# Sum of squares over channels in two fp32r parts, placed behind the first added products; one output product of the last head placed behind that head's own sum

## The chip, the cores and the metric

The kernel is one program on one core of a Trainium2 chip. The metric is the device time of that program in microseconds (us): the median of several runs. Engines are named as in the profile: PE (TensorE, matmuls), PEld (its weight loads, which run beside the matmuls), DVE (VectorE), ACT (ScalarE), POOL (GpSimd), SP (the queue that issues loads).

## The reference, cut to what matters

Two transformer-like blocks in fp32 over x with 1024 tokens and 1024 channels.

```
x = x + concat(pool_mixer, hgrn2_mixer) @ w_out            # first block
h = rms_norm(x, g);  x = x + square(relu(h @ w_up)) @ w_down
x = x + merged @ w_out                                     # second block
h = rms_norm(x, g);  up = dwconv3(h @ w_up);  x = x + (gelu(gate) * val) @ w_down
rms_norm(x, g) = x * rsqrt(mean(x*x over channels) + eps) * g
```

The mean is over channels. Channels lie on the 128 partitions (8 tiles of them), so the squares are first added over the 8 tiles and then over the partitions, by a product with a matrix of ones.

## The kernel before

Each fp32 product is made of three fp32r products: with w = w_hi + w_lo and a = a_hi + a_lo (the high part is a copy into fp32r, the low part the rest of it), PE adds w_hi*a_hi, w_hi*a_lo and w_lo*a_hi in PSUM. ACT makes the high parts of activations, DVE the low parts; for the weights ACT makes high parts and POOL the low ones. Each engine works through an order written out by hand and waits on counting semaphores.

Both up-projections (called stages `mlp` and `ffn`, each one a call of `up_stage` on PE and of `enter` on ACT and DVE) use a Strassen-like scheme: for each pair of output tiles, seven products (`b11, t2, t3, t1, b21, t4, b22`) of 4 row pairs kk, that is 12 matmuls of 128x512 each, so 84 matmuls for a pair. The row pairs are taken in PAIR_ORDER = (0, 1, 3, 2). The factors of h are in part direct (DIRECT: b11, t1, b21, b22) and in part sums (MIXED: t2, t3, t4); each has a sum by DVE, a high part by ACT (`h_combo_hi`, L2402) and a low part by DVE (`h_lows`, L3326 and L3328). The high part of "y" (`..._t_scaled`) is the scaled term from which DVE's three mixed sums (L3310, L3313, L3315) start.

The scale 1/rms is not in h: it is multiplied in when results are read. DVE's first reads of the results (`first_pieces`, L3451; `first_ffn_pieces`, L3809) need it as `rinv`.

The entry of a stage, that is its first pair (`first_pair` on PE), is made of plain products, since the sums are not there yet:
- PE: `begin`/`end` of b11 in banks 6 and 7, `begin` of t1 in banks 0 and 1, then **`sum_features`** (L1482: ones times `sq_sum`, plain fp32, two halves, into banks 4 and 5), then two `add_product`s of 12 matmuls each, then `end`, `add_product`, `end`, `add_product` (30 matmuls), and then pair 2 (`up_pair`), whose b11 waits for `piece_read` (both first pieces read out of banks 6 and 7) and for the low part of its a11.
- ACT (`enter`): last square, `first_sum`, `second_sum`, the high parts of row pair 3 MIXED (y, t2, t3, t4), y of row pair 2, then `inverse` (waits for `norm_summed`; Ln at L2205 out of banks 4 and 5, Exp at L2207, each with a table load ahead of it), then the high parts t2, t3, t4 of row pair 2, then the high parts of pair 2's weights (L2420).
- DVE (`enter`): last addition of squares (L3340), then sums and low parts MIXED of row pair 3, then of row pair 2, then the first pieces.
- POOL (`split_pair`): sums of pair 2's weights (L1294 to L1304), then their low parts (L1318), each behind its high part.

In stage `ffn` DVE also handles the width-3 convolution of the pair before (`tap`, L3839 and L3843), the gelu product (`gated`, L3849) and reads the t1 piece at L3897; PE's last product of a pair, b22, goes into the same bank as t1 and so waits for that read.

The last head (`head(HEADS - 1, ...)`) runs steps of the recurrence, with products of the output projection between them (`begin_out(t, [k])`: output tile t, channel tile k, 6 matmuls of 128x512). Its mean of squares is already made in two fp32r parts: sq_hi by ACT (L2366), sq_lo by DVE (L3270), four matmuls (L1649) behind a wait for `sq_lo_ready`; ACT takes Ln of it (L2368, `o_log`), and the third output tile (`begin_third`) waits for that, as its banks are those of the mean.

`sq_hi_ready` and `sq_lo_ready` are one counter each for the whole program: 6 heads, then two more in the layer norm of the second block.

## Time and profile before

| | us |
|---|---|
| median of 3 runs | 2427.71 (2427.33 to 2430.54) |
| the profiled execution | 2425.44 |
| its span | 2423.6 |

In the page of the profile:

| engine | busy us | share |
|---|---|---|
| PE | 2399.5 | 99% |
| PEld | 1978.9 | 82% |
| DVE | 1890.3 | 78% |
| POOL | 1361.3 | 56% |
| ACT | 959.4 | 40% |

A matmul of 128x512 in fp32r is listed with 389 ns, but consecutive ones start closer together than that, since they are pipelined. In a timeline a row gives the start, the length, the engine, the line, what it writes and reads, and in brackets how long the engine was idle before it and what ended that. In the chain of waits a row gives the start and length of a stretch and what it was spent on.

### The profile page before, as it was taken

The numbers are of one execution on the slowest core, as the hardware profiler recorded it, in microseconds if no ns is written. First come the engines' busy times: TensorE is split into PE (matmuls) and PEld (weight loads), VectorE is DVE, ScalarE is ACT, GpSimd is POOL, SyncE is SP. The second block draws the span as 40 slices with busy tenths as digits, with TensorE's granted clock in tenths as the row PEclk, the third lists the DMA queues.
The fourth block names the chain that finished last, engine by engine and source line by source line (L and its number), as shares of the span: only waits on it lengthen the run. The fifth ranks groups of instructions, "written<-read, shape, count | busy, mean of one in ns | idle before, by whom it ended". The sixth has DMA issues, their size and how long they took to land.

```text
span 2423.6 us, 37422 instructions
## 1 busy us (share of the span) xinstructions
PE 2399.5 (99%) x13845; PEld 1978.9 (82%) x13845; DVE 1890.3 (78%) x1915; ACT 959.4 (40%) x1318; POOL 1361.3 (56%) x792
## 2 busy tenths in 40 slices
PE   8999999999999999999999999999999999999998
PEld 8788887888888788887777788888888888888887
DVE  6766666776667788888877889354799999999998
ACT  5344445353333533324333331310355455443434
POOL 3222222369887767772322223333379999978786
PEclk9999999999999999999999999999999999999999
DMA  6111112234444755431311111113222222235332
GB/s 227 37 35 43 35 35 97 105 122 160 148 155 171 258 172 155 151 126 37 130 42 35 39 35 52 44 52 123 95 87 78 87 86 87 78 129 184 105 118 88
DMA packets 243637, 244.79 MB, mean 101 GB/s; under 512 B 16944, under 2 KB 212187, under 8 KB 238811
## 3 DMA queue, kind: packets, MB, share of 16 engines
q1 hardware_dynamic: 214916, 166.70, 22.1%
q10 hardware_dynamic: 28630, 76.86, 8.3%
q8 instruction: 59, 0.97, 0.2%
q14 instruction: 32, 0.25, 0.0%
HBM read 181.13 MB, written 64.17 MB: 101 GB/s over the span
## 4 chain that ended last, share of the span: by engine, by line
PE 86%; DVE 7%; POOL 2%; ACT 2%; issue 2%; DMA 1%; SPq 0%; DVEq 0%; POOLq 0%; ACTq 0%
PE psum L1455 30%; PE psum L1744 26%; PE psum L1864 11%; PE psum L2112 7%; PE psum L2014 3%; PE psum L1493 2%; PE psum L1580 1%; PE psum L1518 1%; PE psum L1926 1%; PE psum L1945 1%; DVE sq_sum_gain L3583 0%; POOL ffn_s_lo L1318 0%; PE psum L1640 0%; DVE sq_sum L3340 0%; DVE sq_sum L3574 0%
## 5 line engine op out<-in xcount | busy, mean ns | idle before, releaser
L1261 POOL CAST w_hi<-w_raw 128x1024 fp32r<-128x1024 f32 x85 | 98.2, 1156 | 770.3 <-issue 386.4
L1455 PE MATMUL psum<-h_hi,w_hi 128*128 128x512 f32 x1040 | 329.7, 398 | 0.6 <-DVE zg L3074 0.3
L1455 PE MATMUL psum<-h_lo,w_hi 128*128 128x512 f32 x1040 | 321.4, 390 | 0.0
L1455 PE MATMUL psum<-h_hi,w_lo 128*128 128x512 f32 x1040 | 320.7, 390 | 0.0
L1455 PEld LDWEIGHTS psum<-h_hi,w_lo 128*128 128x128 f32 x1040 | 195.2, 188 | 41.9
L1455 PEld LDWEIGHTS psum<-h_lo,w_hi 128*128 128x128 f32 x1040 | 195.2, 188 | 41.6
L1269 POOL TENSOR_TENSOR w_lo<-w_raw,w_hi 128x1024 fp32r<-128x1024 f32 x85 | 221.0, 2601 | 9.6 <-DVE h_lo L3043 2.8
L1455 PEld LDWEIGHTS psum<-h_hi,w_hi 128*128 128x128 f32 x1040 | 189.2, 188 | 38.9 <-issue 2.1
L3637 DVE SCALAR_TENSOR_TENSOR conv_t<-u_t,cols,conv_t 128x1024 f32<-128x1024 f32 x120 | 175.2, 1460 | 2.6
L1318 POOL TENSOR_TENSOR ffn_s_lo<-ffn_s_sum,ffn_s_hi 128x512 fp32r<-128x512 f32 x84 | 159.8, 1931 | 7.0 <-POOL ffn_s_sum L1304 3.5
L1744 PE MATMUL psum<-ffn_t_hi,ffn_s_hi 128*128 128x512 f32 x252 | 98.0, 389 | 0.0
L1744 PE MATMUL psum<-ffn_t_lo,ffn_s_hi 128*128 128x512 f32 x252 | 98.0, 389 | 0.0
L1744 PE MATMUL psum<-ffn_t_hi,ffn_s_lo 128*128 128x512 f32 x252 | 98.0, 389 | 0.0
L1318 POOL TENSOR_TENSOR mlp_s_lo<-mlp_s_sum,mlp_s_hi 128x512 fp32r<-128x512 f32 x60 | 94.9, 1611 | 2.7 <-ACT mlp_s_hi L2420 2.7
L1864 PE MATMUL psum<-down_part_hi,down_hi_odd 128*128 128x512 f32 x228 | 88.8, 390 | 0.3 <-DVE down_x L3501 0.3
L1864 PE MATMUL psum<-down_part_lo,down_hi_odd 128*128 128x512 f32 x228 | 88.7, 389 | 0.0
L1864 PE MATMUL psum<-down_part_hi,down_lo_odd 128*128 128x512 f32 x228 | 88.7, 389 | 0.0
L3493 DVE TENSOR_TENSOR down_part_lo<-down_part_raw,down_part_hi 128x1536 fp32r<-128x1536 f32 (+2 forms) x31 | 71.0, 2291 | 8.5 <-ACT down_part_hi L2556 8.5
L1864 PE MATMUL psum<-down_part_hi,down_hi_even 128*128 128x512 f32 x196 | 76.2, 389 | 0.0
L1864 PE MATMUL psum<-down_part_lo,down_hi_even 128*128 128x512 f32 x196 | 76.2, 389 | 0.0
L1864 PE MATMUL psum<-down_part_hi,down_lo_even 128*128 128x512 f32 x196 | 76.2, 389 | 0.0
L2420 ACT ACTIVATE ffn_s_hi<-ffn_s_sum 128x512 fp32r<-128x512 f32 x84 | 48.4, 624 | 63.8 <-POOL ffn_s_sum L1296 55.7
(626 smaller groups left out, 6857.3 us busy)
## 6 DMA issues: line engine op xcount, KB each, us to landing
w_raw<-in_w_in SPq DMA_DIRECT2D x120, 256.0 KB, 3.0
w_raw<-in_w_up SPq DMA_DIRECT2D x76, 256.0 KB, 3.4
act_parts<-act_mixed ACTq DMA_DIRECT2D x15, 1024.0 KB, 3.8
down_part_raw<-act_parts SPq DMA_DIRECT2D x14, 1024.0 KB, 5.6
down_part_raw<-act_parts SPq DMA_DIRECT2D x15, 768.0 KB, 6.4
ffn_raw<-in_w_up SPq DMA_DIRECT2D x44, 256.0 KB, 3.5
ffn_rows<-ffn_gate ACTq DMA_DIRECT2D x22, 512.0 KB, 2.6
ffn_part_raw<-ffn_rows SPq DMA_DIRECT2D x18, 512.0 KB, 4.5
```

Of the source, the lines that this page charges most:

```text
L1261: pool.tensor_copy(hi, raw).then_inc(weight_hi, 1)
L1269: pool.tensor_tensor(lo, raw, hi.bitcast(F32), ALU.subtract).then_inc(weight_split, 1)
L1318: done = pool.tensor_tensor(lo[:, :], full[c], hi[:, :].bitcast(F32), ALU.subtract)
L1455: last = pe.matmul(psum[:, first_bank + t, :], w, a[:, k, t * HALF:(t + 1) * HALF], start=(k == order[0] and j == 0), stop=(k == order[-1] ...
L1493: last = pe.transpose(psum[:, dst_bank + c // 4, (c % 4) * P:(c % 4 + 1) * P], block_in, ident[:, :])
L1744: last = pe.matmul(psum[:, bank, :], w, a[:, :], start=start and kk == part[0] and j == 0, stop=stop and kk == part[-1] and j == 2, skip_g ...
L1864: done = pe.matmul(psum[:, bank, :], w, b, start=first and i == 0 and k == 0, stop=last and i == len(window) - 1 and k == 2)
L2014: last = pe.matmul(psum[:, bank + t, :], w, a[:, t * HALF:(t + 1) * HALF], start=(k == 0 and j == 0), stop=(k == 3 and j == 2))
L2112: done = pe.matmul(psum[:, bank, 0:tokens.stop - tokens.start], w, b, start=first and i == 0 and k == 0, stop=last and i == len(window) - ...
L2420: act.activation(stage.weights[s][c][0][:, :], src, ACT.Copy).then_inc(weight_combo_hi, 1)
L3493: dve.tensor_tensor(part_lo[f % 3][:, here, :], part_raw[f % 3][:, here, :], part_hi[f % 3][:, here, :].bitcast(F32), ALU.subtract).then_i ...
L3637: dve.scalar_tensor_tensor(acc, u_t[:, c % 2, tap:tap + SEQ], w, acc, ALU.mult, ALU.add)\
```

## The change

- `first_pair` (both stages): `sum_features` is taken out. Behind the two `add_product`s, PE waits for `sq_lo_ready` and makes four fp32r matmuls of `norm_ones` with `norm_hi` and `norm_lo` (two halves each) into the same banks 4 and 5.
- ACT, in `enter`: behind the MIXED high parts of row pair 3 it copies ones into `norm_ones` (128x128) and `sq_sum` into `norm_hi` (128x1024, fp32r); then y of row pair 2 and `inverse` as before.
- DVE, in `enter`: behind the MIXED sums and low parts of row pair 3 it waits for `sq_hi_ready` and makes `norm_lo` = `sq_sum` - `norm_hi` (128x1024), then the MIXED part of row pair 2 as before. `norm_hi` lies where `rinv` lies, `norm_lo` where `sq_sum` lies, `norm_ones` in the free bytes at the end.
- Last head: the product of output tile 1, channel tile 6, is made at the start of `begin_third`, behind the four matmuls of the head's own mean, and not ahead of them.
- Later waits on the two shared counters are raised by the numbers added (`sum_channels`, `out_scaled`, the layer norm).

```diff
@@ buffers
+        norm_ones = at("norm_ones", [P, P], A_END, F32R)
+        norm_hi, norm_lo = (at(f"norm_{n}", [P, SEQ], a, F32R) for n, a in (("hi", A_CONST + 4 * KB), ("lo", A_NORM + 24 * KB)))
@@ PE, last head
             def begin_third():
+                begin_out(1, [6])
                 begin_out(2, range(7))
...
-                             lambda: begin_both((1, 5), (0, 6), (1, 6)), begin_third, lambda: begin_both((1, 0), (0, 1))])
+                             lambda: begin_both((1, 5), (0, 6)), begin_third, lambda: begin_both((1, 0), (0, 1))])
@@ PE, first_pair
                 begin(stage, "a21", "t1", 0)
                 begin(stage, "a11", "t1", 1)
-                sum_features(sq_sum, stage.sums + KT - 1, 4)
                 pe.wait_ge(weight_combo, q * 7 + 7)
                 pe.wait_ge(first_taken, q + 1)
                 add_product(stage, "a12", "b21", 6).then_inc(seventh_done, 1)
                 pe.wait_ge(sum_taken, q * 2 + 2)
                 add_product(stage, "a22", "b21", 7).then_inc(seventh_done, 1)
+                pe.wait_ge(sq_lo_ready, HEADS + (1 if stage is mlp else 4))
+                for j, part in enumerate((norm_hi, norm_lo)):
+                    for t in range(2):
+                        last = pe.matmul(psum[:, 4 + t, :], norm_ones[:, :], part[:, t * HALF:(t + 1) * HALF],
+                                         start=j == 0, stop=j == 1)
+                last.then_inc(norm_summed, 1)
                 end(stage, "a21", "t1", 0)
@@ ACT, enter
                 h_combos_hi(stage, PAIR_ORDER[2], MIXED)
+                act.activation(norm_ones[:, :], ones[:, :], ACT.Copy)
+                act.activation(norm_hi[:, :], sq_sum[:, :], ACT.Copy).then_inc(sq_hi_ready, 1)
                 h_combo_hi(stage, PAIR_ORDER[3], "y")
                 inverse(m, norm, eps)
@@ DVE, enter
-                for kk in PAIR_ORDER[2:]:
-                    h_combos(stage, kk, MIXED)
+                h_combos(stage, PAIR_ORDER[2], MIXED)
+                dve.wait_ge(sq_hi_ready, HEADS + (1 if stage is mlp else 4))
+                dve.tensor_tensor(norm_lo[:, :], sq_sum[:, :], norm_hi[:, :].bitcast(F32), ALU.subtract).then_inc(sq_lo_ready, 1)
+                h_combos(stage, PAIR_ORDER[3], MIXED)
```

## Rows read from the trace of the kernel before

**Rows 1.** The page: granted clock of PE in 40 slices of the span.
```profile
PEclk9999999999999999999999999999999999999999
```
**Rows 2.** Chain of waits, whole span: start us, us, what.
```profile
420.29 68.34 PE psum L1455 x300
488.63 9.52 PE psum L1744 x42
498.15 1.72 PE psum L1482 x4
499.87 284.30 PE psum L1744 x1254
...
1838.81 345.75 PE psum L1744 x1524
```
**Rows 3.** Timeline, end of the last head: ACT, DVE and PE.
```profile
416.25 1.28 ACT L2368 ACT_TABLE_LOAD   x1
416.26 1.23 DVE L3270 TENSOR_TENSOR sq_lo<-e_t,sq_hi 128x1024 fp32r<-128x1024 f32 x1 [5.86 <-ACT sq_hi L2366]
418.02 0.62 PE L1649 MATMUL psum<-sq_hi,ones_r 128*128 128x512 f32 x2
418.47 0.61 PE L1649 MATMUL psum<-sq_lo,ones_r 128*128 128x512 f32 x2
419.13 1.11 ACT L2368 ACTIVATE e_t<-psum,eps 128x1024 f32<-128x1024 f32 x1 [1.60 <-PE psum L1649]
420.29 0.74 PE L1455 MATMUL psum<-h_hi,w_out_hi 128*128 128x512 f32 x2 [1.21 <-ACT e_t L2368]
```
**Rows 4.** Timeline, entry of stage mlp, ACT.
```profile
501.29 0.63 ACT L2402 ACTIVATE mlp_t_hi<-mlp_t_sum 128x512 fp32r<-128x512 f32 x1 [0.55 <-DVE mlp_t_sum L3315]
501.82 0.71 ACT L2402 ACTIVATE mlp_t_scaled<-x_t,cols 128x512 f32<-128x512 f32 x1
...
503.85 1.12 ACT L2205 ACTIVATE rinv<-psum,eps 128x1024 f32<-128x1024 f32 x1
```
**Rows 5.** Timeline, entry of stage mlp, DVE.
```profile
501.23 2.88 DVE L3326 TENSOR_TENSOR mlp_t_lo<-mlp_t_sum,mlp_t_hi 128x512 fp32r<-128x512 f32 x3
504.03 0.74 DVE L3310 SCALAR_TENSOR_TENSOR mlp_t_sum<-x_t,cols,mlp_t_scaled 128x512 f32<-128x512 f32 x1
...
507.96 1.90 DVE L3326 TENSOR_TENSOR mlp_t_lo<-mlp_t_sum,mlp_t_hi 128x512 fp32r<-128x512 f32 x3 [1.62 <-ACT mlp_t_hi L2402]
509.77 1.28 DVE L3451 SCALAR_TENSOR_TENSOR mlp_a<-psum,rinv 128x512 f32<-128x512 f32 x2
```
**Rows 6.** Timeline, entry of stage mlp: POOL, and PE's first matmul of pair 2.
```profile
500.59 1.76 POOL L1304 TENSOR_TENSOR mlp_s_sum<-mlp_raw,mlp_s_sum 128x512 f32<-128x512 f32 x1
509.57 1.44 POOL L1318 TENSOR_TENSOR mlp_a_lo<-mlp_raw,mlp_a_hi 128x512 fp32r<-128x512 f32 x1 [7.22 <-ACT mlp_a_hi L2420]
...
511.99 0.39 PE L1744 MATMUL psum<-mlp_b_hi,mlp_a_hi 128*128 128x512 f32 x1
```
**Rows 7.** Groups by line and shape, ACT: the copy of ones elsewhere.
```profile
L2743 ACT ACTIVATE ln_ones<-ones 128x128 fp32r<-128x128 f32 x1 | 0.3, 290 | 0.0
```
**Rows 8.** Timeline, entry of stage ffn: DVE and ACT.
```profile
1774.92 0.74 DVE L3310 SCALAR_TENSOR_TENSOR ffn_t_sum<-x_t,cols,ffn_t_scaled 128x512 f32<-128x512 f32 x1
...
1774.74 1.12 ACT L2205 ACTIVATE rinv<-psum,eps 128x1024 f32<-128x1024 f32 x1
```
**Rows 9.** Timeline, stage ffn, DVE's t1 reads of pairs 3 to 5, and PE.
```profile
1816.73 0.67 DVE L3897 TENSOR_TENSOR ffn_z_val<-third_sum,psum 128x512 f32<-128x512 f32 x1
...
1838.08 0.68 DVE L3897 TENSOR_TENSOR ffn_z_val<-third_sum,psum 128x512 f32<-128x512 f32 x1
...
1856.79 0.67 DVE L3897 TENSOR_TENSOR ffn_z_val<-third_sum,psum 128x512 f32<-128x512 f32 x1
...
1838.81 0.50 PE L1744 MATMUL psum<-ffn_b_hi,ffn_s_hi 128*128 128x512 f32 x1 [1.44 <-DVE ffn_z_val L3897]
```
**Rows 10.** Timeline, stage ffn: DVE's gelu product of the pair before.
```profile
1819.62 2.26 DVE L3849 TENSOR_TENSOR ffn_gate<-ffn_gate,ffn_val 128x1024 f32<-128x1024 f32 x1 [1.61 <-ACT ffn_gate L2802]
```

More of the change, by code:

```diff
@@ L570, in out_scaled @@
             done = {"act": tile_scaled, "dve": out_ready, "pool": pool_scaled}[by]
-            eng.wait_ge(done, (KT if by == "pool" else HEADS + 2) + OUT_BY[:t + 1].count(by))
+            eng.wait_ge(done, (KT if by == "pool" else HEADS + 4) + OUT_BY[:t + 1].count(by))
         psum = ctx.enter_context(nc.psum_tensor("psum", [P, BANKS, HALF], F32))
@@ L2032, in sum_channels @@
             def sum_channels(hi, lo, nth, first_bank, done):
-                pe.wait_ge(sq_lo_ready, HEADS + nth)
+                pe.wait_ge(sq_lo_ready, HEADS + 1 + nth)
                 for j, part in enumerate((hi, lo)):
@@ L3736, in _ @@
                                   ALU.add).then_inc(ln_added, 1)
-            dve.wait_ge(sq_hi_ready, HEADS + 1)
+            dve.wait_ge(sq_hi_ready, HEADS + 2)
             dve.tensor_tensor(ln_sum_lo[:, :], ln_inv[:, :], ln_sum_hi[:, :].bitcast(F32), ALU.subtract).then_inc(sq_lo_ready, 1)
@@ L3748, in _ @@
                 dve.tensor_tensor(ln_sq[0], ln_sq[0], ln_sq[c], ALU.add).then_inc(ln_added, 1)
-            dve.wait_ge(sq_hi_ready, HEADS + 2)
+            dve.wait_ge(sq_hi_ready, HEADS + 3)
             dve.tensor_tensor(ln_sq_lo[:, :], ln_sq[0], ln_sq_hi[:, :].bitcast(F32), ALU.subtract).then_inc(sq_lo_ready, 1)
```

## The prediction

> **What bounds the kernel now.** I read four views in this order. The chain of waits over the span shows where one engine sets the end: from the end of the last head to deep in stage mlp it is PE alone, product after product, with the fp32 sum as a link of its own [rows 2], and from 1838.81 on the same in stage ffn. In such a stretch a microsecond taken from PE is a microsecond gained, and one of idle PE is lost. 42 products take 9.52 us, so one takes 0.227; 1254 in 284.30 give the same [rows 2]. The timeline around the last head shows a PE that waits 1.21 us for ACT's Ln [rows 3]. The timelines of the two entries show what ACT, DVE and POOL have ready, and when [rows 4 to 8]. The last is stage ffn's pairs 3 to 5: before 1838.81 PE does not set the end there; it waits 1.44 us for DVE's t1 read [rows 9].
>
> **Last head.** Nothing is removed: six matmuls, 6 x 0.227 = 1.36 us, go behind the mean's four. The mean now starts at 418.02, when PE gets to it, though sq_lo is ready at 416.26 + 1.23 = 417.49 [rows 3]. Without the six ahead of it PE would be there at 416.66, so it waits for sq_lo instead and starts near 417.54. Starting again after a wait costs PE about 0.1 us: the two matmuls at 420.29, behind one, are listed with 0.74, those at 418.02, without one, with 0.62 [rows 3]. So Ln starts at 419.13 - 0.48 + 0.1 = 418.75 and ends at 419.87. PE fills that time with the moved product, until about 419.9. The third tile starts at 419.9, not 420.29: **-0.4 us**. Its bounds are 0 (the product's data is late and nothing moves) and -0.5 (no restart cost). The table load ahead of Ln stands at 416.25, right behind sq_hi, and Ln then waits 1.60 for PE: a load is done ahead of the wait [rows 3]. I need that below.
>
> **Entry of stage mlp.** *Removed:* the fp32 sum, 1.72 us of PE [rows 2]. *Added on PE:* four fp32r matmuls, 4 x 0.227 = 0.91. By itself that is -0.81.
> *The new wait.* PE now goes on to the two added products, 24 x 0.227 = 5.44 us, and is through at 498.15 + 5.44 = 503.6 (0.2 earlier for the start of the next, as a listed end lies behind the next start). Is norm_lo there? ACT's last high part of row pair 3 starts at 501.29, the next operation at 501.82 [rows 4]. There norm_ones begins (0.29, [rows 7]), then norm_hi, for which I take the 1.11 of an ACTIVATE of that width [rows 3]; norm_hi is done at about 503.2. DVE's low parts of row pair 3 run from 501.23 to 504.03 [rows 5], so norm_hi is in time and DVE sets it: norm_lo from 504.03 to 505.26, with sq_lo's 1.23 for the same shape [rows 3]. PE waits from 503.4 to 505.3, **1.9 us idle**. All of PE's later work of this entry stands behind that wait. The four matmuls end at 505.3 + 0.1 + 3 x 0.227 + 0.39 = 506.5; PE is free for the 30 remaining ones at 506.3 and would begin pair 2 at 506.3 + 30 x 0.227 = 513.1, where it was 511.99 [rows 6]: +1.1 already.
> *Who waits for the sum.* ACT's Ln starts at 503.85 now [rows 4], behind its table load, long after the sum. It will start at 506.5: its table load is done while it waits, as in the last head. That is 2.65 to 2.7 later. Behind Ln stand, in ACT's order, Exp, the high parts of row pair 2 and the high parts of pair 2's weights; so DVE's low parts at 507.96 [rows 5] and POOL's a11 low part at 509.57 [rows 6] come 2.7 later too. DVE's own new 1.23 is covered: its sums of row pair 2 move from 504.03 to 505.26, end by 507.6, and before they were followed by 1.62 us of waiting for ACT [rows 5]. If that cover were gone, 1.23 would be added once.
> *What PE meets at pair 2.* b11 needs both first pieces read: now at 509.77 + 1.28 = 511.05, then at 513.75 [rows 5]. It needs a11's low part: 509.57 + 1.44 = 511.01, then 513.7 [rows 6]. PE, there at 513.1, waits to 513.8 and restarts at about 0.1: 513.85 against 511.99, **+1.85 us**. After that PE is alone on the chain to 784 [rows 2], so nothing gives it back. Bounds: +1.0 (PE's own time, if the pieces came early enough) and +2.7 (all of ACT's delay).
>
> **Entry of stage ffn.** The same code, with the same distances: DVE is free for norm_lo at 1774.92, so it ends at 1776.15, the four matmuls near 1777.4, and Ln starts there, against 1774.74 [rows 8]: +2.7 for ACT, and +1.85 for PE at pair 2. But here PE is not what sets the end later. Pair 4's b22 waits until 1838.81 for a DVE that runs behind [rows 9], and that DVE is chained to ACT (1.61 us idle for the gelu [rows 10]), ACT to POOL's sums, and POOL to the high parts that stand behind Exp; through this run the 2.7 go on unreduced. PE alone would be at b22 at 1838.81 - 1.44 + 1.85 = 1839.2, the read is done at 1838.76 + 2.7 = 1841.5: the stage moves by **+2.7 us**, and PE's wait grows from 1.44 to 2.3. Bounds: +0.4 (DVE catches up all of it, 1.85 - 1.44) and +2.7 plus one more slow pair, which is a rival below.
>
> **Moved DMAs:** none; the change issues no transfer, and no queue is passed. The raised counts of later waits cost nothing: the same events release them. Banks 4 and 5 are first reused by the next stage's products.
>
> **The skill's price of a table load.** The rows show a load of 1.28 us and the next ACTIVATE at once behind it: Ln ends at 419.13 + 1.11 = 420.24, and such loads sit between Ln and Exp. The Trainium skill, ScalarE: Activation LUTs, "What ACT_TABLE_LOAD costs", puts about 1283 ns on the load and a further 1380 on a drain, 2.66 in all. By it a load hidden in the wait would hide twice as much and Ln's delay would be some 1.4 less in each stage. The load's 1283 ns agrees with this trace, the drain is not in it, and the sum goes by the trace.
>
> **Sum.** -0.4 + 1.85 + 2.7 = +4.15, call it +4.2 us. Against the profiled execution's own 2425.44 that is 2429.6. That execution was 2.3 under the median of the three runs; I carry the difference over to the median: 2427.71 + 4.2 = **2431.9 us**, +0.17%. A difference under 0.2% (4.9 us) can't be told from none here.
>
> **The rivals.**
> - *The sum is covered, and the gain is what PE saves.* Then PE gains 0.81 twice and 0.4 in the head: -2.0, 2425.7. It needs norm_lo at 503.4 instead of 505.26. For it: the last square sum is ready long before. Against it: DVE's own order, full from 501.23 to 504.03 [rows 5]. Chance 0.05.
> - *Stage ffn takes only what PE loses.* DVE catches up before pair 4; its pairs can take 18.7 us (1838.08 to 1856.79 [rows 9]) where PE's take 84 x 0.227 = 19.05, and with PE later DVE waits less for it. Then the stage costs +0.4 to +1.1 and the total is about +2.1, 2429.8. Against it: that idle time of 1.61 waits for ACT, not PE. Chance 0.17.
> - *Slower: the slow pair repeats.* Pair 3 to 4 took DVE 1838.08 - 1816.73 = 21.35 us, the next 18.7 [rows 9]; the difference, 2.6, is what DVE's two-input operations lose when they meet POOL's, together with the wait for the gelu [rows 10]. With ACT, DVE and POOL 2.7 later against PE, DVE's reads can fall behind a POOL operation for one pair more. It decides when the t1 read of pair 5 ends more than 19.05 us behind that of pair 4. Price +2.6: total +6.8, 2434.5. For it: DVE is busy throughout there, and the first low part of row pair 3 in [rows 5], three of which take 2.88 where three later ones take 1.90, loses 1.0 while POOL is in its 1.76 us operation at 500.59 [rows 6]. Against it: everything on these three engines shifts together, and POOL is idle from 502.35 to 509.57, around norm_lo. Chance 0.18. The Trainium skill, SBUF — State Buffer, "SBUF: two separate sides", says that a DVE operation with two SBUF inputs and a GpSimd one take a common port in turn, each for its whole length; the lost 1.0 agrees, and norm_lo is such an operation, so by that rule too it is the meeting that counts and not the work.
> - *The idle 1.9 us lowers PE's clock.* The granted clock is full in all 40 slices, the one with the 1.21 us wait among them [rows 1]. I give it less than 0.02 and put it into the slower side.
>
> **How the numbers follow.** Forecast 0.6, rivals 0.05, 0.17, 0.18. The forecast's own range is +3.2 to +5.4 (the two restarts, 0.2 on norm_lo's start, and a median of a few runs that itself moved by up to 3 us): 2430.5 to 2433.5. Its upper part passes 4.9, some 0.2 of the 0.6. So slower is 0.2 + 0.18 = 0.38, faster 0.03, same 0.59. For 8 in 10 the range goes down to the weaker stage ffn and up to the repeated slow pair: 2427.8 to 2434.8.
>
> **What would show it.** In the changed profile: four matmuls with norm_hi and norm_lo of 0.39 us each; PE idle some 1.9 us ahead of them in both stages, released by DVE norm_lo; norm_lo of 1.23 right behind the third low part; ACT's table load ahead of a wait of 1.4 us or so and Ln 2.7 later against the entry's start; a PE wait of about 0.7 at the first matmul of pair 2; in stage ffn a wait of 2 to 2.5 at pair 4's b22; in the last head the third tile 0.4 earlier. The forecast is wrong if PE finds norm_lo ready, if the wait at b22 of ffn's pair 4 has shrunk, or if a wait at L3897 shows up in pair 5.

## The result, and the profile after

The changed kernel took 2432.49 us (median of 10 runs, 2431.03 to 2435.53) against 2427.27 us of the kernel before in the same session (10 runs, 2425.13 to 2433.01): ratio 1.0023, 95% interval [1.0015, 1.0031], +5.2 us. The forecast was 2431.9 with a range of 2427.8 to 2434.8 and a difference of +4.2. The changed kernel, run a second time in a later session, gave 2432.15 against 2426.89 (1.0019 [1.0010, 1.0028]). So it is slower by about 5 us. The prediction drew the bound between "same" and "slower" at 0.2% (4.9 us), and both intervals contain it; the point of the ten runs is just beyond, on the side to which the prediction gave 0.38 and not 0.59.

In the one profiled execution of each, the span went from 2423.6 to 2430.5 us, +6.9. By marks that exist in both traces it comes about so:

| from the mark | to the mark | before | after | difference |
|---|---|---|---|---|
| start of the span | sq_lo of the last head | 416.26 | 417.30 | +1.04 |
| sq_lo | third output tile's first product | 4.03 | 3.71 | -0.32 |
| there | last addition of squares, stage mlp | 73.41 | 73.34 | -0.07 |
| there | PE's first product of pair 2, mlp | 18.29 | 20.63 | +2.34 |
| there | last addition of squares, stage ffn | 1252.59 | 1253.39 | +0.80 |
| there | b22 of pair 4, ffn | 74.23 | 77.31 | +3.08 |
| there | end | 584.79 | 584.82 | +0.03 |

The first row lies ahead of everything that was changed, and the fifth between the two entries, where the chain of waits after shows a transfer of activations for the down-projection (`down_part_raw<-act_parts`, 7.79 us at 789.99) that it does not show before. Neither came back in the experiments below in a fixed size (between the entries it is 1252.3 to 1254.9 us over all traces, 1252.6 before), so I don't count them to the change. The change's own three rows give -0.32 + 2.34 + 3.08 = **+5.1 us**, which agrees with the timed runs.

**The last head.** The timeline of the changed kernel (start us, us, engine, line, operation, and in brackets the idle time before it with what ended it), DVE, ACT and PE in turn:

```profile
417.30 1.22 DVE L3280 TENSOR_TENSOR sq_lo<-e_t,sq_hi 128x1024 fp32r<-128x1024 f32 x1 [5.86 <-ACT sq_hi L2374]
...
417.28 1.28 ACT L2376 ACT_TABLE_LOAD   x1
419.83 1.12 ACT L2376 ACTIVATE e_t<-psum,eps 128x1024 f32<-128x1024 f32 x1 [1.26 <-PE psum L1651]
...
418.58 0.74 PE L1651 MATMUL psum<-sq_hi,ones_r 128*128 128x512 f32 x2 [0.70 <-DVE sq_lo L3280]
...
421.01 0.71 PE L1457 MATMUL psum<-h_hi,w_out_hi 128*128 128x512 f32 x2
```

As in [rows 3], with everything 1.04 us later. PE now reaches the mean before sq_lo is there and waits 0.70 us; in return the moved product stands behind the mean and fills the time of Ln, and the 1.21 us wait ahead of the third tile is gone. The third tile comes 3.71 us behind sq_lo's start, where it was 4.03.

**Entry of stage mlp.** First the chain of waits of the changed kernel, from the third low part to pair 2 (start us, us, what):

```profile
501.28 0.64 ACT mlp_t_hi L2410
...
502.81 2.38 DVE mlp_t_lo L3336 x2
505.19 1.15 DVE norm_lo L3372
...
506.38 1.21 PE psum L1798 x4
...
507.62 1.12 ACT rinv L2213
...
513.63 1.21 DVE mlp_a L3463 x2
...
514.98 5.05 PE psum L1747 x21
```

In [rows 2] this stretch was PE alone. Now the chain leaves PE, runs over DVE's low parts to norm_lo, the four matmuls, ACT's Ln, back to DVE and only at 514.98 to PE again. The timeline of the same stretch, ACT:

```profile
501.28 0.63 ACT L2410 ACTIVATE mlp_t_hi<-mlp_t_sum 128x512 fp32r<-128x512 f32 x1 [0.55 <-DVE mlp_t_sum L3325]
501.82 0.29 ACT L2473 ACTIVATE norm_ones<-ones 128x128 fp32r<-128x128 f32 x1
502.02 1.04 ACT L2474 ACTIVATE norm_hi<-sq_sum 128x1024 fp32r<-128x1024 f32 x1
502.97 0.71 ACT L2410 ACTIVATE mlp_t_scaled<-x_t,cols 128x512 f32<-128x512 f32 x1
503.69 1.28 ACT L2213 ACT_TABLE_LOAD   x1
507.62 1.12 ACT L2213 ACTIVATE rinv<-psum,eps 128x1024 f32<-128x1024 f32 x1 [2.64 <-PE psum L1798]
```

DVE and POOL:

```profile
501.22 3.97 DVE L3336 TENSOR_TENSOR mlp_t_lo<-mlp_t_sum,mlp_t_hi 128x512 fp32r<-128x512 f32 x3
505.12 1.21 DVE L3372 TENSOR_TENSOR norm_lo<-sq_sum,norm_hi 128x1024 fp32r<-128x1024 f32 x1
...
511.73 1.90 DVE L3336 TENSOR_TENSOR mlp_t_lo<-mlp_t_sum,mlp_t_hi 128x512 fp32r<-128x512 f32 x3 [3.17 <-ACT mlp_t_hi L2410]
513.55 1.28 DVE L3463 SCALAR_TENSOR_TENSOR mlp_a<-psum,rinv 128x512 f32<-128x512 f32 x2
...
502.30 1.74 POOL L1306 TENSOR_TENSOR mlp_s_sum<-mlp_raw,mlp_s_sum 128x512 f32<-128x512 f32 x1
513.34 1.44 POOL L1320 TENSOR_TENSOR mlp_a_lo<-mlp_raw,mlp_a_hi 128x512 fp32r<-128x512 f32 x1 [9.30 <-ACT mlp_a_hi L2428]
```

and PE:

```profile
506.38 0.73 PE L1798 MATMUL psum<-norm_hi,norm_ones 128*128 128x512 f32 x2 [2.15 <-DVE norm_lo L3372]
506.95 0.63 PE L1798 MATMUL psum<-norm_lo,norm_ones 128*128 128x512 f32 x2
...
514.98 0.47 PE L1747 MATMUL psum<-mlp_b_hi,mlp_a_hi 128*128 128x512 f32 x1 [0.59 <-DVE mlp_a L3463]
```

Against [rows 4 to 6] three things are to be seen. The third group of low parts takes 3.97 us, not 2.88, since it meets one more of POOL's weight sums: POOL's last one stands at 502.30 where it was at 500.59, 1.71 later, of which the stage's own shift is 0.65. (norm_lo is late by less than the 1.1 us that the group is longer: counted from the last addition of squares, the group starts 0.66 earlier than before, since the first of DVE's three sums, 1.43 us before, now takes 0.75 and misses POOL.) norm_lo follows it, and PE, done with the added products, is idle 2.15 us for it. ACT has its table loaded by 504.97 and then waits 2.64 us: Ln, Exp, the high parts, POOL's and DVE's parts behind them all come 3.1 us later, and PE waits once more, 0.59, at pair 2.

**Stage ffn.** The same entry, and pair 4's b22, on PE:

```profile
1780.40 0.73 PE L1798 MATMUL psum<-norm_hi,norm_ones 128*128 128x512 f32 x2 [2.19 <-DVE norm_lo L3372]
...
1788.99 0.47 PE L1747 MATMUL psum<-ffn_b_hi,ffn_a_hi 128*128 128x512 f32 x1 [0.59 <-DVE ffn_z_val L3821]
...
1845.68 0.50 PE L1747 MATMUL psum<-ffn_b_hi,ffn_s_hi 128*128 128x512 f32 x1 [1.98 <-DVE ffn_z_val L3909]
```

and ACT's Ln and DVE's t1 reads of pairs 4 and 5:

```profile
1781.63 1.12 ACT L2213 ACTIVATE rinv<-psum,eps 128x1024 f32<-128x1024 f32 x1 [2.64 <-PE psum L1798]
...
1844.95 0.68 DVE L3909 TENSOR_TENSOR ffn_z_val<-third_sum,psum 128x512 f32<-128x512 f32 x1
...
1863.68 0.68 DVE L3909 TENSOR_TENSOR ffn_z_val<-third_sum,psum 128x512 f32<-128x512 f32 x1
```

The prediction's path to b22 can be read from the chain of waits of the kernel before, stage ffn (pieces of it; start us, us, what), with POOL's row of the changed kernel's timeline last:

```profile
1778.14 1.66 ACT ffn_t_hi L2402 x3
...
1780.47 1.45 POOL ffn_a_lo L1318
...
1818.54 1.05 ACT ffn_gate L2802
...
1787.36 1.43 POOL L1320 TENSOR_TENSOR ffn_a_lo<-ffn_raw,ffn_a_hi 128x512 fp32r<-128x512 f32 x1 [9.30 <-ACT ffn_a_hi L2428]
```

The chain goes from Ln over ACT's high parts to POOL, which from then on has hardly a gap, to ACT's gelu and DVE. From POOL's first low part to b22 it is 58.34 us before (1838.81 - 1780.47) and 58.32 after (1845.68 - 1787.36). Compared with [rows 9], b22's wait grew from 1.44 to 1.98, and the restart is 64.05 us behind Ln (1845.68 - 1781.63), as it was before (1838.81 - 1774.74 = 64.07): the delay of Ln arrives there unreduced. Pair 4 to pair 5 takes 18.73 us: there is no second slow pair.

### The profile page after: what moved, and what is told of

It reads as the page before. It is cut to its first block, busy times and chain, and to the rows that moved or that the text cites. A ratio compares the mean times of both kernels' runs of the same rounds, so it can differ in the third digit from the quotient of the medians.

```text
span 2430.5 us, 37428 instructions
## 1 busy us (share of the span) xinstructions
PE 2401.2 (99%) x13845; PEld 1980.5 (81%) x13845; DVE 1890.3 (78%) x1917; ACT 961.1 (40%) x1322; POOL 1362.1 (56%) x792
## 4 chain that ended last, share of the span: by engine, by line
PE 85%; DVE 9%; ACT 3%; issue 2%; DMA 1%; POOL 1%; SPq 0%; DVEq 0%; ACTq 0%; POOLq 0%
PE psum L1457 28%; PE psum L1747 27%; PE psum L1872 11%; PE psum L2120 7%; PE psum L2022 3%; PE psum L1495 2%; PE psum L1582 1%; PE psum L1520 1%; PE psum L1953 1%; PE psum L1934 1%; DVE sq_sum L3350 1%; DVE sq_sum_gain L3595 0%; PE psum L1642 0%; DVE x_t L3358 0%; DVE ffn_t_lo L3336 0%
```

## The experiments

"Marks" are distances in us from the start of the last addition of squares of a stage, so that the start of the run doesn't enter them. Each comes from one profiled execution. Of the kernels themselves:

| kernel | Ln mlp / ffn | pair 2 mlp / ffn | b22 (its wait) | difference of medians, ratio |
|---|---|---|---|---|
| before | 10.15 / 10.16 | 18.29 / 18.24 | 74.23 (1.44) | |
| changed | 13.27 / 13.26 | 20.63 / 20.62 | 77.31 (1.98) | +5.2, 1.0023 [1.0015, 1.0031] |

**The three parts of the change, each alone.** The first has the head's move only:

```diff
             def begin_third():
+                begin_out(1, [6])
                 begin_out(2, range(7))
...
-                             lambda: begin_both((1, 5), (0, 6), (1, 6)), begin_third, lambda: begin_both((1, 0), (0, 1))])
+                             lambda: begin_both((1, 5), (0, 6)), begin_third, lambda: begin_both((1, 0), (0, 1))])
```

> The kernel before with the last head's product moved, and nothing else. My theory: the head's mean starts when sq_lo is ready and not when PE gets to it, so ACT's Ln comes some 0.4 us earlier against the head's earlier steps and the third output tile starts 0.35 to 0.45 us earlier against sq_hi; PE waits about 0.7 us for sq_lo and no longer for Ln. Time: -0.4 us (2427.3 becomes 2426.9), ratio 0.9998. Rival (the restart and the later product take it all back): 0.0 us and the third tile no nearer to sq_hi.

The second and third have the sum in parts in one stage only (`if stage is mlp` or `if stage is ffn` around the copies, norm_lo and the four matmuls, the other stage keeping its fp32 sum), and no move in the head.

> The kernel before with the two-part sum in stage mlp alone; stage ffn and the head as before. My theory: PE idle about 2 us for norm_lo and 0.6 us at the first product of pair 2; that product starts 1.9 to 2.3 us later against the last addition of squares than before (18.3 us behind its start before), and stage ffn as before (1.4 us wait at pair 4's b22). Time: +1.9 to +2.3 us, ratio 1.0008 to 1.0010. Rival (stage mlp has slack behind the entry that takes it back): pair 2 starts 2 us later, the down-projection does not, 0 us.

> The kernel before with the two-part sum in stage ffn alone. My theory: the whole delay of ACT's Ln reaches the end, through POOL, ACT's gelu and DVE's t1 read: PE's restart at pair 4's b22 comes 2.7 to 3.1 us later against the last addition of squares (74.2 us behind its start before). Time: +2.7 to +3.1 us, ratio 1.0011 to 1.0013. Rival (only what PE loses counts): +1.0 us or less, the wait at b22 gone or shorter.

| kernel | Ln mlp / ffn | pair 2 mlp / ffn | b22 (its wait) | difference of medians, ratio |
|---|---|---|---|---|
| e1_head_only | 9.48 / 10.58 | 18.29 / 18.24 | 74.66 (1.86) | -0.5, 0.9998 [0.9989, 1.0007] |
| e2_mlp_only | 12.94 / 10.27 | 20.30 / 18.23 | 74.35 (1.55) | +2.2, 1.0007 [0.9998, 1.0016] |
| e3_ffn_only | 10.30 / 13.45 | 18.29 / 21.23 | 77.49 (1.70) | +3.1, 1.0013 [1.0004, 1.0022] |

The three add up to -0.5 + 2.2 + 3.1 = +4.8 of the +5.2. Each of these differences is known to some 2 us only, and those of e1 and e2 can't be told from no change; only e3's can. What speaks for the three terms is the marks: the third tile 3.68 us behind sq_lo instead of 4.03, pair 2 of stage mlp later by 2.0, b22 later by 3.3. That stage ffn costs more than stage mlp shows in the marks; the timed intervals of e2 and e3 overlap and don't show it.

The unedited entries in this table say how far one mark can be trusted. With the fp32 sum in its old place Ln stands anywhere from 9.48 to 10.58 and b22 from 74.23 to 74.66, so a mark of one trace is good to about half a us. And e3's pair 2 in stage ffn, 21.23 and without a wait, is not comparable with the changed kernel's 20.62: 0.6 us behind the restart at its four matmuls this execution has a stretch of half clock (last section), and from norm_lo to Ln it is 2.94 us where the changed kernel has 2.50.

**What is it in the entry: the place, the low parts, or the split?** This kernel is the one before with nothing split and no move in the head; only the fp32 sum is moved to where the change has it:

```diff
-                sum_features(sq_sum, stage.sums + KT - 1, 4)
                 pe.wait_ge(weight_combo, q * 7 + 7)
...
                 add_product(stage, "a22", "b21", 7).then_inc(seventh_done, 1)
+                sum_features(sq_sum, stage.sums + KT - 1, 4)
```

> The kernel before with the plain fp32 sum moved behind the two added products in both stages: no new wait, PE's work unchanged. My theory (the late Ln costs, not only PE's idle time): PE is not idle in the entry; the sum ends near 505.4 and Ln starts 1.6 us later than before; pair 2 of stage mlp starts 0.8 us later, stage ffn's b22 of pair 4 1.6 us later. Time: +2.4 us, ratio 1.0010. Rival (what costs is PE idle ahead of the new wait and nothing else): 0.0 us.

Measured: 2430.8 against 2427.43, +3.4, 1.0009 [1.0000, 1.0018]; Ln at 11.63 / 11.60, pair 2 at 18.98 / 18.95, b22 at 75.66 with a wait of 2.01. So moving the sum behind the added products alone delays Ln by 1.5 us, and by the marks it costs 0.69 at pair 2 of stage mlp and 1.43 at b22, +2.1, with no idle PE at the sum. That is less than half of the +5.4 (2.34 + 3.08) that the change costs in the two entries; the splitting, which was to make PE's part shorter, adds the rest. (The timed +3.4 is more than the marks give, as with e5 below; the last section comes back to it.)

The next keeps the changed kernel but takes norm_lo out of the way; PE waits for norm_hi and adds it twice:

```diff
-                pe.wait_ge(sq_lo_ready, HEADS + (1 if stage is mlp else 4))
-                for j, part in enumerate((norm_hi, norm_lo)):
+                pe.wait_ge(sq_hi_ready, HEADS + (1 if stage is mlp else 4))
+                for j, part in enumerate((norm_hi, norm_hi)):
...
-                dve.wait_ge(sq_hi_ready, HEADS + (1 if stage is mlp else 4))
-                dve.tensor_tensor(norm_lo[:, :], sq_sum[:, :], norm_hi[:, :].bitcast(F32), ALU.subtract).then_inc(sq_lo_ready, 1)
+                dve.sem_inc(sq_lo_ready, 1)
```

> The changed kernel without norm_lo: DVE does not make it, PE waits for norm_hi alone and adds it twice, so the mean that scales both stages' results is twice the sum of the high parts and not the sum. PE's four matmuls, ACT's two copies and the place of the sum are as in the changed kernel. My theory (the wait for norm_lo is most of the loss): norm_hi is ready 8.7 us behind the start of the last addition of squares, PE gets to the sum at 9.7, so it doesn't wait; Ln at 10.8 (13.3 in the changed kernel, 10.15 before), pair 2 of stage mlp at 18.05 (before 18.29), pair 4's b22 of stage ffn 0.65 later than before. Time: 0.0 us against before, ratio 1.0000. Rival (the added copies and the late place of the sum cost by themselves): +2 us or more.

Measured: 2428.96 against 2426.61, +2.35, 1.0008 [1.0000, 1.0017]. The interval just reaches no change, but the marks speak against the expected 0: Ln is at 11.31 / 11.46, pair 2 of stage mlp at 18.66 behind a wait of 1.09 (expected: 18.05), b22 at 75.52 (2.00). ACT's timeline of e5_no_low, stage mlp:

```profile
502.40 0.29 ACT L2473 ACTIVATE norm_ones<-ones 128x128 fp32r<-128x128 f32 x1
502.60 1.04 ACT L2474 ACTIVATE norm_hi<-sq_sum 128x1024 fp32r<-128x1024 f32 x1
503.55 0.71 ACT L2410 ACTIVATE mlp_t_scaled<-x_t,cols 128x512 f32<-128x512 f32 x1
504.27 1.28 ACT L2213 ACT_TABLE_LOAD   x1
505.57 1.12 ACT L2213 ACTIVATE rinv<-psum,eps 128x1024 f32<-128x1024 f32 x1
```

Nothing waits here. Ln is late by 1.2 us because the two new copies, from 502.40 to 503.55, stand ahead of it in ACT's own queue. Not all of the 1.2 is theirs, though: in e6 below ACT waits for PE and not for the copies, and Ln is at 10.82, 0.67 late by the place of the sum alone. The copies add some 0.5 to that. Where PE's wait goes, ACT's copies are next, and the stages are still slower than before. The prediction placed the copies in time, to see whether norm_hi is there for norm_lo, and put no price on these 1.15 us of ACT, on which everything behind Ln hangs; in the changed kernel the wait for norm_lo covers them.

**Is norm_lo late for its work or for meeting POOL?** The changed kernel, with POOL's weight sums of pair 2 held back until norm_lo is done:

```diff
+                    pool.wait_ge(sq_lo_ready, HEADS + (1 if stage is mlp else 4))
```

> The changed kernel, with POOL's weight sums of pair 2 held back until norm_lo is done. Theory (DVE is late with norm_lo because its mixed sums and low parts meet POOL's operations): DVE's sums take 0.75 each and not 1.67, its three low parts 1.9 and not 3.97, norm_lo starts 7.0 us behind the start of the last addition (10.8 in the changed kernel), PE doesn't wait, Ln at 10.8; POOL's sums end at about 15.1 and are in time for the high parts. Time: 0.0 us against before, ratio 1.0000. Rival (DVE's and ACT's own order sets norm_lo): norm_lo at 10 or later, +4 us or more.

Measured: 2427.51 against 2426.61, +0.9, 1.0001 [0.9993, 1.0010]: no slowdown can be told from none. DVE's timeline of e6_pool_held, stage mlp, and POOL's first sum:

```profile
498.13 0.75 DVE L3326 SCALAR_TENSOR_TENSOR mlp_t_sum<-x_t,cols,mlp_t_sum 128x512 f32<-128x512 f32 x1
498.96 1.90 DVE L3337 TENSOR_TENSOR mlp_t_lo<-mlp_t_sum,mlp_t_hi 128x512 fp32r<-128x512 f32 x3
501.06 1.23 DVE L3373 TENSOR_TENSOR norm_lo<-sq_sum,norm_hi 128x1024 fp32r<-128x1024 f32 x1 [0.20 <-ACT norm_hi L2475]
...
502.58 1.51 POOL L1297 TENSOR_TENSOR mlp_s_sum<-mlp_raw 128x512 f32<-128x512 f32 x1 [15.89 <-DVE norm_lo L3373]
```

DVE's sum at 498.13 takes 0.75 us where the changed kernel's same sum at 499.52 took 1.67, the three low parts 1.90 instead of 3.97, and norm_lo starts at 7.19 instead of 10.77. PE does not wait at the four matmuls; ACT waits 1.76 us for them ahead of Ln. Ln stands at 10.82 / 10.77, pair 2 at 18.18 / 18.13, b22 at 74.83 with a wait of 1.98. So PE gets back 0.1 us at pair 2, where it waits 0.59, and b22 is still 0.6 late. The rival that norm_lo is simply one operation too many on DVE falls.

**Versions that might beat both.** The first is the kernel before with the head's move and the fp32 sum one place *earlier*, between the two begun products, Ln and Exp ahead of row pair 3's mixed high parts (PAIR_ORDER[2] is row pair 3, where the expectation of e11_early_again says row pair 2). The head's part of the edit is e1's; the rest:

```diff
                 begin(stage, "a21", "t1", 0)
-                begin(stage, "a11", "t1", 1)
                 sum_features(sq_sum, stage.sums + KT - 1, 4)
+                begin(stage, "a11", "t1", 1)
...
-                h_combos_hi(stage, PAIR_ORDER[2], MIXED)
-                h_combo_hi(stage, PAIR_ORDER[3], "y")
+                h_combo_hi(stage, PAIR_ORDER[2], "y")
                 inverse(m, norm, eps)
+                for name in MIXED:
+                    h_combo_hi(stage, PAIR_ORDER[2], name)
+                h_combo_hi(stage, PAIR_ORDER[3], "y")
```

> A version meant to beat both: the kernel before with the head's move, the plain fp32 sum one step earlier (between the two begins of t1) and ACT's Ln and Exp ahead of the mixed high parts of row pair 3, in ACT's idle 3.3 us. Theory (ACT's late Ln is on the path of stage ffn only through what stands behind it): Ln at 4.2 us behind the start of the last addition (before 10.15), the high parts of pair 2's weights 2.5 us earlier, pair 2 of stage mlp unchanged at 18.3, and the 1.44 us wait at stage ffn's pair 4 gone. Time: -0.35 - 1.44 = -1.8 us, ratio 0.9993. Rival (DVE is late at b22 for its own work): the wait stays, -0.4 us.

Measured: 2425.13 against 2426.61, -1.5, 0.9993 [0.9984, 1.0001]. Its ACT timeline, stage mlp:

```profile
498.96 1.12 ACT L2206 ACTIVATE rinv<-psum,eps 128x1024 f32<-128x1024 f32 x1 [0.30 <-PE psum L1482]
...
506.88 1.68 ACT L2403 ACTIVATE mlp_t_hi<-mlp_t_sum 128x512 fp32r<-128x512 f32 x3 [2.25 <-DVE mlp_t_sum L3316]
```

Ln is at 4.15 instead of 10.15, and the high parts of row pair 2 at 12.07 (506.88 - 494.81) instead of 507.24 - 493.70 = 13.54. They now wait for DVE's sums and not for Ln. Pair 2 is where it was (18.28 / 18.22), the b22 wait is gone, and b22 is at 72.98.

The second tries the same with the changed kernel's parts: norm_hi first of all on ACT, norm_lo ahead of DVE's mixed sums, the four matmuls ahead of the added products, the inverse early.

> The changed kernel with its two parts made first: norm_hi on ACT ahead of second_sum, norm_lo on DVE ahead of the mixed sums, in its idle 1.46 us, the four matmuls ahead of the two added products (the place of the sum before), and Ln and Exp ahead of the mixed high parts of row pair 3. Theory: norm_lo is done 3.6 us behind the start of the last addition, PE gets to the sum at 4.3 and doesn't wait, so the 0.81 us that the two-part sum saves on PE are kept in stage mlp (pair 2 at 17.5, before 18.29), Ln at 5.4, and pair 4's b22 of stage ffn 1.3 us earlier than before. Time: -0.35 - 0.8 - 1.3 = -2.5 us, ratio 0.9990. Rival (DVE's later start of the mixed sums, by 0.9 us, and ACT's extra copy push the rest back): 0 us or slower.

Measured: 2425.97 against 2426.61, -0.6, 0.9996 [0.9987, 1.0004]; Ln 5.39 / 6.03, pair 2 at 17.43 / 18.08, but b22 at 74.31 with a wait of 1.67. PE's gain at pair 2 of stage mlp is there. In stage ffn most of it is not: there norm_lo itself meets POOL's first sum and takes 2.33 us instead of 1.23, and PE waits 0.42 for it. The b22 wait stays because ACT's high parts of row pair 2 now wait for DVE (2.34 us in stage mlp, 1.85 in stage ffn), whose sums norm_lo has pushed back; they start at 13.55 in stage ffn, where it was 13.57.

This kernel also shows what b22 really follows. Ln is 4.1 us earlier than before and b22 is not. From the start of the high parts of row pair 2 to b22 it is 60.65 to 60.76 us in all ten traces in which PE waits at b22, this one (60.76) among them; from Ln to b22 it is 64.05 to 64.08 in nine of them, and 68.28 here. Ln counts only as long as the high parts behind it wait for it.

The third starts from e8_parts_first and does DVE's mixed sums of both row pairs ahead of their low parts, and both scaled rows ahead of Ln (DVE's part of the edit):

```diff
-                h_combos(stage, PAIR_ORDER[2], MIXED)
-                h_combos(stage, PAIR_ORDER[3], MIXED)
+                for kk in PAIR_ORDER[2:]:
+                    h_sums(stage, kk, MIXED)
+                for kk in PAIR_ORDER[2:]:
+                    h_lows(stage, kk, MIXED)
```

> The version with the parts made first, and in addition the y of row pair 2 ahead of Ln on ACT, and on DVE the mixed sums of both row pairs ahead of the low parts of both. Theory (that version kept stage ffn's wait because ACT's high parts of row pair 2 waited 2.3 us for DVE's sums): ACT starts the high parts of pair 2's weights 12.4 us behind the start of the last addition of squares (15.1 before and there), the wait at pair 4's b22 is gone, b22 at 72.0 (before 74.2), pair 2 of both stages at 17.4. Time: -0.35 for the head, -0.8 in stage mlp, -2.2 in stage ffn: -3.4 us against before, ratio 0.9986. Rival (DVE and POOL meet for longer and the pieces come late): a wait at pair 2 and no more than -1 us.

Measured: 2431.88 against 2426.89, +5.0, 1.0016 [1.0007, 1.0025]: a clear miss. DVE's and PE's timelines of e9_sums_first, stage mlp, with PE's row of stage ffn last:

```profile
506.06 6.99 DVE L3339 TENSOR_TENSOR mlp_t_lo<-mlp_t_sum,mlp_t_hi 128x512 fp32r<-128x512 f32 x6
512.98 1.28 DVE L3468 SCALAR_TENSOR_TENSOR mlp_a<-psum,rinv 128x512 f32<-128x512 f32 x2
...
514.40 0.47 PE L1748 MATMUL psum<-mlp_b_hi,mlp_a_hi 128*128 128x512 f32 x1 [2.35 <-DVE mlp_a L3468]
...
1788.68 0.47 PE L1748 MATMUL psum<-ffn_b_hi,ffn_a_hi 128*128 128x512 f32 x1 [2.85 <-DVE ffn_z_val L3826]
```

The high parts did come earlier, and the b22 wait went. But six low parts in a row take 6.99 us, 1.17 each instead of the 0.63 of three alone (1.90), because they now lie beside POOL's low parts, which start at 507.61. DVE reads the first banks only behind them, at 512.98 instead of e8_parts_first's 509.94, and PE, which needs those banks, waits 2.35 and 2.85 us; pair 2 is at 20.53 / 20.38. In stage ffn this execution also has a stretch of half clock 1.3 us behind that restart (last section): from pair 2 to b22 it takes PE 56.15 us, and 54.76 in e7, neither with a wait at b22. What was pulled ahead had to be paid for by what stood behind it.

**The changed kernel once more**, unedited, to see which marks hold.

> The changed kernel again, for a second profile. Theory: Ln and the restart at pair 4's b22 in stage ffn stay 64.05 us apart, as in all profiles so far (10.16 and 74.23 before, 13.26 and 77.31 after, 10.77 and 74.83 with POOL held back), and Ln moves with the start of POOL's weight sums, which lies 2.3 to 3.0 us behind the start of the last addition of squares whatever the kernel: the earlier POOL is, the earlier norm_lo (10.3 to 10.8) and Ln (12.8 to 13.3). Time: +5.2 us against before, ratio 1.0022. Rival (POOL's later start belongs to the change): POOL at 2.9 or later in both stages again.

Measured: 2432.15 against 2426.89, +5.3. From Ln to b22 it is 78.33 - 14.27 = 64.06 us in stage ffn, as expected. norm_lo goes with POOL's start: over the six entries with these parts behind the added products and POOL free, POOL's first sum at 2.37 (e10), 2.38 (e2), 2.43 (e3), 2.91 and 3.02 (changed), 3.46 (e10, ffn) stands with norm_lo at 10.45, 10.45, 10.51, 10.77, 10.77 and 10.94. In the rows, what ends POOL's idle time is a transfer that lands (the spill of x or the weight's own), nothing that the change orders. That Ln in e10's stage ffn is 1.0 later than in the first run is only to 0.17 norm_lo's; from norm_lo to Ln it is 3.34 us instead of 2.50, and the clock was at half from 0.07 us behind PE's restart. This run also showed something else, below.

**The best version again, and without the head's move.** The last two are e7_early_inverse unedited, and the same with the second tile's seventh product where the kernel before has it.

> The kernel of e7_early_inverse once more: against before, the head's moved product, and in both stages the fp32 sum of squares between the two begun products, the inverse's two activations ahead of row pair 2's mixed high parts. Two terms make it: the head -0.35, and stage ffn's wait for the gelu's t1 read, 1.44 us in the profile of before, which was gone in e7's. Theory 1 (those waits are all): median 1.4 to 1.8 us under before, ratio 0.9993, as the first time. Theory 2 (besides them, TensorE's waits of 1.8 to 2.9 us are followed in some executions by a stretch of half clock that costs another 1.6 to 2.6 us, and before's timed executions, median 2427, are above its profiled 2425.4 because some have one): this kernel has no wait of 1.4 us or more behind x_added, so nearly all its executions should lie within 2 us of its lowest, its median 1.5 to 2.5 under before, and the profile should show no half-clock stretch between 490 and 2400 us. An outcome within 0.5 us of before would take e7's gain for an accident.

> The same without the head's move (the second tile's seventh product stays where before has it). What the head's move is worth on its own, for e1 could not tell it from no change: third tile's first product 4.03 us behind the start of sq_lo instead of 3.68 to 3.71, so 0.3 us over e11_early_again in the profile counted from that mark; median 0.3 over e11's, 1.1 to 1.5 us under before, ratio 0.9995. If the head's 0.70 us wait for sq_lo, which the move opens, costs more than the 0.35 it saves later, this kernel is as fast as e11 or faster.

| kernel | third tile | Ln mlp / ffn | median (range) | before | ratio |
|---|---|---|---|---|---|
| e11_early_again | 3.72 | 4.16 / 4.09 | 2425.61 (2423.48 to 2431.96) | 2427.15 | 0.9994 [0.9985, 1.0002] |
| e12_early_no_head | 4.05 | 4.16 / 4.08 | 2425.33 (2424.17 to 2425.73) | 2427.15 | 0.9991 [0.9982, 1.0000] |

The gain of 1.5 us came back and the b22 wait was absent both times. The profile of e11 shows no half-clock stretch between 490 and 2400 us, as expected. That nearly all of its executions would lie within 2 us of its lowest was wrong: 7 of 12 don't. The third tile's 0.33 us is in the marks, but in time e12, without the move, is 0.3 us *under* e11, so what the head's move brings is smaller than these runs can tell; that e12's runs lie in 1.6 us and e11's in 8.5 is seen and not explained. Both medians are under the kernel before's, by 1.5 and 1.8 us, with intervals that reach 1.0002 and 1.0000, so that a gain over the kernel before is likely and not shown by either alone, and some 7 us under the changed kernel's, by way of the kernel before.

## Why the prediction was right, and where it was off

- **What bounds the kernel, and the sign.** Right: PE alone between the last head and stage mlp's down-projection, and stage ffn's b22 hanging on ACT's chain. The marks of e2 and e3 show both stages later by about the amounts that those two readings give; of the timed differences only e3's is clear of none.
- **Last head, -0.4.** Measured -0.32 by the marks (-0.35 in e1); no timed run can tell it from nothing. The wait for sq_lo and the restart of 0.1 are both in the rows (0.70, and 0.74 against 0.62).
- **Stage mlp, +1.85.** Measured +2.34 (e2: +2.0). The step that was off is "DVE is free for norm_lo at 504.03": the three low parts took 3.97 us, not the 2.88 copied from [rows 5]. Counted from the last addition of squares norm_lo came 0.44 later than forecast, Ln 0.47, pair 2 0.49. The 2.88 was itself a meeting with POOL, caught at one moment of a POOL whose first sum starts from 2.3 to 3.5 us behind that mark in the traces of these two kernels; I noted the meeting for a rival and priced the main line as if it were fixed. e6, where the meeting is gone, gives 1.90.
- **Ln behind the sum, table load in the wait.** Right in kind: load at 503.69, then 2.64 us idle. The forecast wait was 1.4; Ln was late by 0.47 more, and ACT was through with its copies and the load 0.9 earlier than forecast, the copies taking 1.15 us instead of 1.4 and the last high part of row pair 3 starting 0.66 earlier. No drain shows behind either load, here or in e5, where Ln starts 1.30 us behind the start of its load.
- **Not foreseen:** ACT's two copies. In the changed kernel they are covered by norm_lo, and the sum did not suffer; but "PE's wait is the price" would have misled anyone who mended only the wait. e5 is that mending, and it is still +2.35. Had I listed what is late next once norm_lo is in time, two entries would have stood there: the sum's later place, 0.67 us on Ln (e6), and ACT's 1.15 us of copies, which bring it to 1.16 (e5).
- **Stage ffn, +2.7, unreduced.** Measured +3.08, again 0.4 from norm_lo. The delay of Ln arrives unreduced, as forecast: from Ln to b22 it is 64.0 to 64.1 us in the kernels before, changed, and e1 to e6, over the path by POOL that the prediction named. The wait at b22 was 1.98 and not 2.3, since PE itself came later than forecast (pair 2 +2.38 and not +1.85).
- **Sum.** +4.15 forecast, +5.1 by the profile's own marks and +5.2 by the runs: two terms of 0.4 to 0.5, the same mis-sized one in either stage. The forecast's own range, +3.2 to +5.4, held it. That the median missed 2431.9 by only 0.6 is in part luck: the kernel before took 0.4 us less in the ten runs beside it than in the three runs that the forecast started from.
- **Rivals.** *The sum is covered* did not happen, but e6 shows what it would have taken: POOL out of the way. Even then it gives no gain, since the sum's later place keeps Ln 0.67 late, and with it the first reads and b22; that takes back what PE saves. *Stage ffn takes only what PE loses* falls with the 64.05 us. *The slow pair repeats* falls: pair 4 to 5 took 18.73 us.
- *The idle time lowers PE's clock*, under 0.02: this one I took too lightly, as the last section shows. It is not what made the change slower in its own profile, where no entry shows it.

The rule of the Trainium skill, SBUF — State Buffer, "SBUF: two separate sides", that DVE operations with two SBUF inputs and GpSimd's take a common port in turn, agrees with the rows shown here: 0.75 and 1.67 us for one and the same DVE operation, without and with POOL beside it.

## What to carry to other kernels

When work is moved behind other work on the bounding engine, follow the *result* and not the engine: here 1.7 us of PE work became 0.9, and everything that hangs on the sum came 3.1 us later. For each engine along that path write down what is late next once the first wait is gone; the mending of e5 and the over-reaching of e9 both failed at the second item of such a list. And a duration that was measured beside another engine's work is a range, not a number: here its end moved with the landing of a transfer.

## What the hardware showed beside

**Short stretches at half clock.** In 14 profiled executions PE came back 28 times, between 380 and 1850 us, from a wait of 1.83 to 2.85 us. Within 1.6 us of 11 of these restarts the granted clock fell from 1.00 to 0.50, from the 2.4 to the 1.2 GHz level, and some 3.4 us later it was back at 1.00. It did not fall behind any of the 6 waits of 1.37 to 1.70 us in the same stretch of the runs and up to 2360 us, nor behind the waits for the first transfers at the start of the span (up to 5.4 us). (Behind PE's last product, in the last few us of the span, it is at 0.50 in every trace.) e10_after_again has two, one at each norm_lo wait. Its windows, stage ffn, whose restart is at 1780.07 (from and to us, length; busy us and count of PE, PEld, DVE, ACT, POOL; granted clock; share of DMA; GB/s):

```profile
1778.00:1780.00 2.00, 0.00 (x0) 0.00 (x0) 2.00 (x4) 0.66 (x1) 0.00 (x0) 1.00 0.00 0
1780.00:1782.00 2.00, 1.93 (x5) 1.54 (x6) 1.93 (x4) 0.00 (x0) 0.00 (x0) 0.54 0.00 0
1782.00:1784.00 2.00, 2.00 (x7) 1.58 (x6) 0.25 (x1) 1.84 (x2) 0.00 (x0) 0.61 0.00 0
1784.00:1786.00 2.00, 2.00 (x10) 1.62 (x10) 0.00 (x0) 1.99 (x3) 0.00 (x0) 1.00 0.00 0
```

The same view of e1_head_only around b22 (restart at 1839.60 behind 1.86 us):

```profile
1840.00:1842.00 2.00, 2.00 (x8) 1.57 (x7) 2.00 (x2) 0.56 (x2) 2.00 (x3) 0.69 0.00 0
1842.00:1844.00 2.00, 2.00 (x7) 1.51 (x6) 1.97 (x3) 0.63 (x1) 2.00 (x2) 0.50 0.31 127
1844.00:1846.00 2.00, 2.00 (x10) 1.67 (x9) 1.97 (x3) 1.17 (x2) 2.00 (x2) 0.96 0.33 135
```

The cost can be read right behind b22. From its first matmul to the sixtieth behind it it is 13.73 to 13.77 us in the seven traces with a wait and no such stretch there (before, changed, e2, e3, e6, e8, e10), and 15.34 or 15.35 in e1, e4 and e5, which have one: it costs 1.6 us, and hundreds of matmuls on the difference is still 1.6. Not every late end is the clock's: behind b22 e1 loses another 1.0 us and e3, without a stretch there, 3.5, with waits of 0.90 at 2213 and of 1.37 at 2359 and longer tails. In the entries a stretch costs what it takes from the four matmuls and from PE's way to pair 2: from norm_lo to Ln 0.84 us more in e10's stage ffn and 0.44 in e3's, nothing in e10's stage mlp, where the clock fell only 1.4 us behind the restart; pair 2 stands at 21.66, 21.23 and 21.17, where the changed kernel had 20.62. The changed kernel's own profile has one, at 386, ahead of sq_lo; from that restart to sq_lo it is 31.61 us, and 31.65 in the trace before, so there it cost nothing. The 40 slices of the page [rows 1] are 60 us wide and show nothing of it. The Trainium skill, TensorE: Matmul & The Clock Gate, "Part 1: The HAM clock gate", tables two states of this clock, 1.2 and 2.4 GHz; the inner windows (0.50 and 1.00) agree.

This could account for part of the spread of the timed runs, and where it happens it makes a wait of 2 us dearer than its length. How much of the +5.2 is of this kind stays open: the changed kernel has three such waits behind the last head and the one before has none, but the marks without any half clock already give +5.1, and the interval of the timed runs, +3.6 to +7.5, doesn't tell +5.1 from +6. e4 and e5, whose timed differences (+3.4, +2.35) are 1.0 to 1.3 above what their marks give (+2.1, +1.3), would fit such an extra, but the intervals of both reach down to their marks, and no experiment shows it alone.

**One engine's start is another's duration.** Starting POOL's sums 6 us later (e6) delayed nothing that the marks of pair 2 show and brought norm_lo 3.6 us earlier, without removing one instruction.
